# RMS norms of a two-layer diffusion backbone: the reciprocal root moved from the operand to the matmul result

## The reference, cut to what matters

```
rmsnorm(x, g)  = x * rsqrt(mean(x*x) + EPS) * g
modulate(x)    = rmsnorm(x, g) * (1 + scale) + shift      # scale, shift: one value per channel and group
proj           = modulate(x) @ w_in
conv_ffn       = (silu(g) * v) @ w_down,  g, v = split(dwconv3(modulate(x) @ w_up) + conv_b)
```

## Time and profile before

| | before |
|---|---|
| time, median of 3 runs | 2189.38 us (2186.27 to 2192.53) |
| profiled execution: span, first to last instruction | 2179.9 us |
| PE busy | 1991.0 us (91%) |
| DVE busy | 1154.7 us (53%) |
| POOL busy | 1152.3 us (53%) |
| ACT busy | 670.4 us (31%) |

### The profile page before, as it was taken

How to read it: one execution, slowest core, us unless ns; L and a number is a source line. 1 busy time by engine, 2 the same in 40 slices (tenths; PEclk the granted TensorE clock), 3 DMA queues, 4 the chain that set the end, 5 groups by cost and what they waited for, 6 DMA issues and landing times. The chain is left out here.

```text
span 2179.9 us, 33056 instructions
## 1 busy us (share of the span) xinstructions
PE 1991.0 (91%) x12945; PEld 1864.4 (86%) x12945; DVE 1154.7 (53%) x1505; ACT 670.4 (31%) x1093; POOL 1152.3 (53%) x437
## 2 busy tenths in 40 slices
PE   5789887989999999998999999997697999999997
PEld 3678776878899889997998999896696999999997
DVE  4655575667634653354647676768614452452353
ACT  4334332233211320121356464647201220120121
POOL 3233323535567556776454444440474777777763
PEclk8899988989999999999999999998798999999999
DMA  8211116524434522224143333322321222222221
GB/s 275 100 45 53 36 34 209 183 92 144 151 110 124 155 87 68 74 59 128 39 120 116 97 106 97 101 75 87 107 68 48 68 73 72 77 67 78 68 63 73
DMA packets 292913, 208.60 MB, mean 96 GB/s; under 512 B 7344, under 2 KB 284885, under 8 KB 292309
## 3 DMA queue, kind: packets, MB, share of 16 engines
q1 hardware_dynamic: 292821, 207.32, 31.2%
HBM read 196.63 MB, written 10.67 MB: 95 GB/s over the span
## 5 line engine op out<-in xcount | busy, mean ns | idle before, releaser
L828 POOL TENSOR_SCALAR w_hi<-raw 128x1024 fp32r<-128x1024 f32 (+1 forms) x216 | 629.7, 2915 | 983.5 <-PE ps L859 909.8
L859 PE MATMUL ps<-h_hi,w_hi 128*128 128x322 f32 (+1 forms) x2304 | 559.9, 324 | 22.3 <-DVE h_lo L1702 22.0
L859 PE MATMUL ps<-h_lo,w_hi 128*128 128x322 f32 (+1 forms) x2304 | 533.8, 313 | 0.0
L859 PE MATMUL ps<-h_hi,w_lo 128*128 128x322 f32 (+1 forms) x2304 | 533.1, 313 | 0.0
L831 POOL TENSOR_TENSOR w_lo<-raw,w_hi 128x1024 fp32r<-128x1024 f32 (+1 forms) x216 | 522.2, 2418 | 18.0
L859 PEld LDWEIGHTS ps<-h_hi,w_hi 128*128 128x128 f32 x2304 | 391.2, 192 | 51.0 <-issue 33.4
L859 PEld LDWEIGHTS ps<-h_hi,w_lo 128*128 128x128 f32 x2304 | 394.5, 191 | 0.0
L859 PEld LDWEIGHTS ps<-h_lo,w_hi 128*128 128x128 f32 x2304 | 391.5, 191 | 0.0
L859 PE MATMUL ps<-g_hi,w_hi 128*128 128x322 f32 (+1 forms) x816 | 190.4, 315 | 10.3 <-DVE g_lo L1956 10.3
L859 PE MATMUL ps<-g_lo,w_hi 128*128 128x322 f32 (+1 forms) x816 | 188.7, 313 | 0.0
L859 PE MATMUL ps<-g_hi,w_lo 128*128 128x322 f32 (+1 forms) x816 | 188.2, 312 | 0.0
(11 more groups left out here) (295 smaller groups left out, 2533.2 us busy)
## 6 DMA issues: line engine op xcount, KB each, us to landing
ada<-in_ada_w SPq DMA_DIRECT2D x48, 1024.0 KB, 5.3
raw<-in_ffn_w_up SPq DMA_DIRECT2D x88, 512.0 KB, 3.9
raw<-in_ssd_w_in SPq DMA_DIRECT2D x40, 512.0 KB, 4.1
R<-scr_acs SPq DMA_DIRECT2D x40, 512.0 KB, 4.8
raw<-in_ffn_w_down SPq DMA_DIRECT2D x32, 512.0 KB, 3.8
raw<-in_att_w_in SPq DMA_DIRECT2D x16, 512.0 KB, 6.1
raw<-in_ssd_w_out SPq DMA_DIRECT2D x16, 512.0 KB, 4.0
raw<-in_ffn_w_down SPq DMA_DIRECT2D x16, 384.0 KB, 3.4
```

The source lines that it names most:

```text
L828: nc.gpsimd.tensor_scalar(w_hi[j % 2][:, 0:k, :], raw[j][:, 0:k, :], 1.0, None, ALU.mult).then_inc(w_hi_done, 1)
L859: ins = mm(out[:, cols], w[slot][:, k, :], x[:, k_of(k), cols], start=first and k == 0 and i == 0, stop=last and k == n - 1 and i == 2)
```

## The change

- The root no longer goes into h. `h_hi` = x * gain (ScalarE, `high`) and `h_lo` = x * gain - h_hi (VectorE, `low`) are written behind each residual update. The root is broadcast into an SBUF row (`rrow`) and multiplied onto the matmul result.
- The two pad columns move together to columns 128 and 129 and hold the shift of the two groups, so that two columns of each result are `shift @ w`. The eviction adds them: as bias of the middle tap or silu, while the side taps see `-shift @ w` in the pads.
- `ss` now runs after k-step 5 of the projection's first tile, `norm_rb` after k-step 3 of its second one (in attention: halfway through the first).
- Evictions: in attention q, k, v are read by VectorE (times root) and then ScalarE adds the bias in SBUF; in FFN and SSD VectorE first scales the slot in place (`scale`), copies two pad columns and forms two biases, and only then ScalarE reads it, in two instructions instead of one.
- The modulation steps are reordered (`ADA_ORDER`), gains are formed pair by pair. `high` and `low` of norm 0 stand inside the chain of steps 1 to 7. Step 8's weights are no longer loaded early but after attention, and step 9's behind the read-back of `xT`. Steps 16 to 19 move to output tiles 4 and 5.
- SSD: the dt work moves by about one tile, state and y updates are done in PSUM or in place instead of over a temporary (`y2`).

```diff
-W = NP_ + 1 + NS + 1
+W = NP_ + 2 + NS
-S0 = NP_ + 1
+S0 = NP_ + 2
+PADS = slice(NP_, S0)
+ADA_ORDER = (4, 5, 6, 7, 0, 1, 2, 3, 8, 16, 9, 17, 10, 18, 11, 19, 12, 13, 14, 15)
-        ADA_B = ((8, 9), (10, 11), (12, 13), (14, 15), (16,), (17,), (18,), (19,))
+        ADA_B = ((8, 9), (10, 11), (12, 13), (14, 15), (16, 17), (18, 19), (), ())
...
-    put(0, 1, "dtT", 0)
-    put(3, 1, "sum", 0)
-    put(4, 1, "acsT", 0)
+    put(2, 0, "dtT", 0)
+    put(4, 1, "sum", 0)
+    put(5, 1, "acsT", 0)
...
@@ SyncE, behind attention
+            ada(8)
+            sp.dma_start(xT[:, :, :], scr_x).then_inc(x_back, 16)
             ada(9)
-            sp.dma_start(xT[:, :, :], scr_x).then_inc(x_back, 16)
...
@@ TensorE, FFN
+                            def row(k, half=half):
+                                if half == 0 and k == 5:
+                                    ss(n_)
+                                if half == 1 and k == 3:
+                                    norm_rb(n_)
...
@@ ScalarE
+            def high(n, k):
+                act.wait_ge(gain_done, k // 2 + 1 + 4 * n if n < 2 else 7 + n)
+                hi, _ = h_at_k(n, k)
+                for s_, cols in SEGS:
+                    ins = A_(hi[:, cols], xT[:, k, cols], ACT.Copy, scale=gain1[:, n, k, s_:s_ + 1])
+                ins.then_inc(h_hi_done, 1)
             for s in range(1, 8):
                 ada_high(s)
+                if 2 <= s < 6:
+                    high(0, 2 * (s - 2))
+                    high(0, 2 * (s - 2) + 1)
...
-                            act.wait_ge(mm_done, 2 * i + (tp + half + 1))
+                            act.wait_ge(ffn_v, 2 * i + (2 * f0 + half + 1))
...
-                            A_(buf[:, :], acc(half), ACT.Identity, bias=param_at(m + bcol),
-                               scale=param_at(m + (wc + 44))).then_inc(ffn_id, 1)
+                            for s_, cols in ((0, slice(0, S0)), (1, slice(S0, W))):
+                                b_ = 24 + 2 * half + s_
+                                ins = A_(buf[:, cols], acc(half)[:, cols], ACT.Identity, bias=small[:, b_:b_ + 1],
+                                         scale=param_at(m + (wc + 44)))
+                            ins.then_inc(ffn_id, 1)
...
@@ VectorE
+            def low(n, k):
+                dve.wait_ge(gain_done, k // 2 + 1 + 4 * n if n < 2 else 7 + n)
+                dve.wait_ge(h_hi_done, 8 * n + k + 1)
+                hi, lo = h_at_k(n, k)
+                for s_, cols in RANGES:
+                    ins = stt(lo[:, cols], xT[:, k, cols], gain1[:, n, k, s_:s_ + 1], f32(hi[:, cols]), ALU.mult,
+                              ALU.subtract)
+                    (step(ins) if s_ == 0 else ins.then_inc(h_ready, 1))
+            def scale(slot, n):
+                step(tt(acc(slot), acc(slot), rrow(n)[:, :], ALU.mult))
+                step.wait()
+            def side_pads(slot):
+                step(cp(acc_wide(slot)[:, 0:W + 2:W + 1], acc(slot)[:, PADS]))
             for s in range(1, 8):
                 if s < 7:
                     ada_low(s + 1)
                 ada_row_out(s)
                 mod_evac(s - 1, 0)
+                if s < 5:
+                    gain(0, s, slice(2 * s - 2, 2 * s))
+                if 2 <= s < 6:
+                    low(0, 2 * (s - 2))
+                    low(0, 2 * (s - 2) + 1)
...
+                        tt((q_raw, k_raw, v_raw)[i][:, :], src, rrow_att[:, :], ALU.mult).then_inc(acc_free_dve, 1)
...
+                            dve.wait_ge(mm_done, 2 * i + (tp + half + 1))
+                            if isinstance(i, int) and (p, i, half) == (0, 0, 0):
+                                row(n_)
+                            scale(half, n_)
+                            side_pads(half)
+                            ts(small[:, 24 + 2 * half:26 + 2 * half], acc(half)[:, PADS], nw, pcol_at(m + bc_), ALU.mult,
+                               ALU.add).then_inc(ffn_v, 1)
                             dve.wait_ge(ffn_id, 2 * i + (2 * f0 + half + 1))
...
@@ VectorE, SSD y update
-                        tt(h64(y2[:, :]), h64(bank(b)), per_head(eacs, c, d_, g), ALU.mult).then_inc(ssd_free_dve, 1)
-                        ins = tt(y_, y_, y2[:, :], ALU.add)
+                        chain(tt(h64(bank(b)), h64(bank(b)), per_head(eacs, c, d_, g), ALU.mult))
+                        tt(y_, y_, bank(b), ALU.add).then_inc(ssd_free_dve, 1)
```

More of the change, by code:

```diff
@@ L849, in _, with steps @@
             mm, tr = nc.tensor.matmul, nc.tensor.transpose
-            def steps(t, slot, aslot, x_hi, x_lo, ks, k_of=lambda k: k, first=True, last=True, n=KD, ready=None):
+            def steps(slot, aslot, x_of, ks, first=True, last=True, n=KD, ready=None, after=None):
                 out = acc(aslot)
@@ L966, in _ @@
                         pe.wait_ge(x_spilled, 16)
-                    ins = steps(t, t % 2, t % 2, h_hi, h_lo, (2 * q, 2 * q + 1), ready=h_wait(0) if t == 0 else None)
+                    if t == 0 and q == 2:
+                        norm_rb(0)
+                    ins = steps(t % 2, t % 2, h_of(0), (2 * q, 2 * q + 1), ready=h_wait(0) if t == 0 else None)
                     if q == 3:
@@ L1074, in pair @@
                             pe.wait_ge(acc_free_dve, dve_accs(ap) + 2 * i + half - 2)
-                            steps(t, half, half, h_hi, h_lo, range(KD),
-                                  ready=h_wait(n_) if peeled and p == 0 and half == 0 else None
-                                  ).then_inc(mm_done, 1)
+                            begins = peeled and p == 0
+                            def row(k, half=half):
[3 more added lines that the diff above has]
+                                    norm_rb(n_)
+                            steps(half, half, h_of(n_), range(KD), ready=h_wait(n_) if begins and half == 0 else None,
+                                  after=row if begins else None).then_inc(mm_done, 1)
                             if ada:
@@ L1121, in y_part @@
                         pe.wait_ge(*acc_free(A_O + half - 2))
-                    ins = steps(None, half, half, y_hi, y_lo, (k % KD,), k_of=lambda _: k, first=part == 0,
-                                last=part == 1)
+                    ins = steps(half, half, y_of(part), (k % KD,), first=part == 0, last=part == 1)
                     if k % KD == KD - 1:
@@ L1266, in so_pair @@
                             pe.wait_ge(acc_free_dve, 2 * i + (half + dve_accs(A_O) - 2))
-                        steps(None, half, half, y_hi, y_lo, range(KD), k_of=lambda k: 8 * part + k, first=part == 0,
-                              last=part == 1).then_inc(mm_done, 1)
+                        steps(half, half, y_of(part), range(KD), first=part == 0, last=part == 1).then_inc(mm_done, 1)
             for k in range(12, 16):
@@ L1609, in _ @@
             A_(small[:, 8:13], small[:, 0:5], ACT.Sqrt).then_inc(yr_root, 1)
-            def so_squares(i):
-                for half in range(2):
-                    square(3, 2 * i + half, (so_x, 2 * i + (half + 1)), sq[half][:, :])
-            so_squares(0)
-            with act.Fori(1, 4) as i:
-                so_squares(i)
-            norm(3)
+            act.wait_ge(x_back, 32)
+            for hi, i, _, _, k0, k1 in H2_PADS:
+                ins = A_(hi[:, i:i + k1 - k0, PADS], mod[:, 72 + k0:72 + k1, :], ACT.Copy)
+            ins.then_inc(shift_hi, 1)
+            for m in range(KD):
+                square(3, m, (so_x, m + 1), sq[m % 2][:, :], before=True)
+                if m == 7:
+                    A_(h_hi[:, 7, PADS], mod[:, 79, :], ACT.Copy).then_inc(shift_hi, 1)
+            root(3)
             ffn(1, T_F1, A_F1)
@@ L2212, in _ @@
+            low(3, 7)
+            dve.wait_ge(shift_hi, 5)
+            tt(h_lo[:, 7, PADS], mod[:, 79, :], f32(h_hi[:, 7, PADS]), ALU.subtract).then_inc(shift_lo, 1)
             add_square(3, 7, sq[1])
-            norm(3)
             ffn(1, T_F1, A_F1)
```

520 lines of the change are left out of this document (314 added, 206 removed).

## The result

After: 2217.72 us median of 4 runs (2212.05 to 2218.10); before, on the same chip: 2187.82 us (2179.93 to 2192.53). The ratio is 1.0133, 95% interval 1.0112 to 1.0153. I had forecast 2174 us and a range up to 2198: wrong in sign and outside the range. The profiled execution took 2217.51 us with a span of 2215.7. So only 1.8 us lie around a span; most of the 9.5 us that the prediction put there was that the profiled execution of before was a short one.

A forecast was written before the change was run, and what follows sets the result against it. TensorE, 91% busy, was taken to bound the kernel with its dense work plus holes. Terms -38.8 + 3 + 6.5 + 3 + 0 + 11 = -15.3 us gave 2174 us, own range 2164 to 2184, 8 in 10 2155 to 2198.

The forecast's parts named there:

- Norms 1 to 3: TensorE's holes at these norms mostly close, as h is written behind each residual: 13.5, 10.8 and 14.5 us won, together -38.8.
- the hole only moves: Rival at the norms: the second tile waits for the broadcast as the first did; 2184 us, chance 0.11.
- Norm 0 and its chain: Start of the kernel: no gain, first tile ends near 93 against 89.9; term +3 us, bounds -12 and +8.
- Steps 8 and 9: Modulation behind attention: weights land later, step 9's behind the read-back of `xT`; term +6 us, bounds 0 and +10.
- Steps 16 to 19: Modulation steps run in pairs; term +0.5 us.
- Attention: Evictions: VectorE gets 12 scalings of about 0.86 us, partly hidden; term +3 us, bounds 0 and 10.
- FFNs: Evictions take 1.5 us longer per tile, hidden with 7.1 to spare; term 0 for 44 pairs.
- the cover of `hm`: FFN pairs with modulation keep 0.5 us of cover; rival that it fails: +18 us, 2192 us, chance 0.10.
- SSD: Net 64 us more on VectorE, mostly hidden; 3 us in each of three groups plus 2 us: +11, bounds -5 and +32.
- in-order waits between VectorE and ScalarE at each conv tile: Rival in SSD: they put half of the 64 us on TensorE's path, +32; 2197 us, slower, chance 0.15.
- the 14.7 us credited for the lock: SSD y update: VectorE no longer held by GpSimd's lock, 32 x 0.46 = -14.7 us of its work.
- waits for freed slots over 20 us: Sign against the forecast: it fails as a whole if PE's waits for freed slots sum to more than 20 us.

The follow-up runs named there:

- tenth run: The changed kernel with VectorE's scaling, side pads and bias left out in the second FFN; median 1.3 us below the changed kernel's.
- twelfth run: The kernel before with only the y update multiplied in place in PSUM; 2182.65 us beside 2185.84 for before, ratio 0.9987.
- fourth: The changed kernel with norm 2 alone done as in the kernel before, but the dt chain's polynomial one tile later than there; 25 us less.
- fifth run: The changed kernel with norm 2 and the dt chain as in the kernel before, and modulation steps 16 to 19 spread; 2176.6 us.
- third: The changed kernel with VectorE's two side taps of each SSD conv tile, from the second group on, behind the next scan work; 3.4 us more.
- sixth: The changed kernel with the SSD dt chain moved later, off the first conv tiles; 6 us less by medians.
- seventh: The changed kernel with the side taps of the b and c tiles alone put behind the next scan event; 7.8 us less by medians.
- eighth run: The changed kernel with steps 16 to 19 spread, the dt chain later, and the b and c taps behind the next scan event; 2201.0 us.

## Why the prediction was wrong

- *Norms 1 to 3*: right. Forecast -38.8; measured -12.7, -13.9 and -14.6, -41.2 in all. That norm 1 came within 1 us of its forecast is partly luck: it holds 4.2 us at tiles 26 to 28 for which seven other kernels with the same code there have 0.6, and 9.1 us at tiles 59 to 65, where its modulation pair now stands, for which the prediction had 3. That the hole only moves is refuted by norm 3's two waits of 2.29 and 1.68 us.
- *Norm 0 and its chain*: the steps were right, the end a little off. `ada_hi(3)` to (6) were forecast at 47.0, 54.1, 61.1 and 68.1; they started at 45.7, 53.6, 60.3 and 67.0; the timeline of ACT has the period with the two pairs of `high`:

```profile
45.72 1.89 ACT L1402 ACTIVATE ada_hi<-ada 128x2048 fp32r<-128x2048 f32 x1
51.77 1.92 ACT L1430 ACTIVATE h_hi<-xT,gain 128x128 fp32r<-128x128 f32 x4 [4.16 <-DVE gain L1785]
53.60 1.90 ACT L1402 ACTIVATE ada_hi<-ada 128x2048 fp32r<-128x2048 f32 x1
```

  The last turn started at 79.0 for 81 to 82, and tile 0 ended 0.7 us earlier than before, not 3 later; since tile 0 lies between -2.9 and +4.2 us in the other kernels, +3 is not refuted.
- *Steps 8 and 9*: right (+6.8 for +6), with the cause that was named: putting step 9 ahead of the read-back removed the jump at tile 17, though 4.3 us came back at the next one.
- *Steps 16 to 19*: the term of +0.5 failed, at +12.6. I counted the steps' work and not their transfers' due times: a pair was already the tightest pattern at output tiles 1 to 3, and two more pairs in a row left no tile in which the two buffers could refill. Spreading them took 8.8 of the 12.6 us away.
- *Attention*: -1.2 for +3. The same code cost +5.3 us in four other kernels, so this term is neither shown right nor wrong.
- *FFNs*: the cover of `hm` held through 44 pairs (lag flat), but the term of 0 is 10.5 us in the profile (3.9 and 6.6), at first tiles and passes between parts. The 2.2 us of tiles 65 to 91 repeat in every changed kernel; much of the rest comes and goes between kernels with the same code there. What the tenth run shows to be the scaling's, 2.0 us at tile 150, lies in norm 3's stretch, where the prediction had 1.7 for it.
- *SSD*: the term that decided. Its mechanism stood in the prediction as a rival: in-order waits between VectorE and ScalarE at each conv tile, which decides once more than 26 of the 64 us show. Of the stage's 49 us, 37.5 went with the scaling. (The rival's sum is 8.7, not 8.6, and gives 2198 us, not 2197.) These sizes were off. First, "3 us of PE waits in each of three groups": a group cost 11.4 us on average, since lateness goes on from the b tile to the x tiles (6.0, 6.6 and 5.4 us at the border and 4.4, 4.4 and 3.3 on the next three tiles), where I counted one border. Second, the slow matmuls behind each wait, 2.3 us of a border's 6.0, were in no term. Third, the 14.7 us credited for the lock bought nothing in the kernel before (twelfth run), and with the scaling 12.2 of them came back on two neighbours. And "2 us where the dt chain meets the first tiles" was 14.9: 5.4 went with the scaling, and putting the chain's series back by one tile took 10.4 off the first tiles (fourth to fifth run). Its pieces moved one tile later, which the diff shows and I read as harmless.

So the step that failed is the prediction's "there I expect 3 us of PE waits in each of three groups; plus 2 us where the dt chain meets the first tiles": +11 us, where the runs show 49, the scaling 37.5 of them and the places of the dt chain most of the rest. How the 37.5 split into added work and a longer way through each eviction stays open.

The error of 51 us (forecast -15.3, measured +35.8 by spans) is SSD 38, steps 16 to 19 12, FFNs 10.5, less 9 us by which start, attention and norms went better.

What the prediction named as tests came out so: no wait over 3 us between the last output tile and the third tile at norms 1 to 3 (1.8, 0.9 and 2.3 us at most, right), `ss` inside the first tile (right), the last turn after 80 us (79.0, just wrong), one PE wait for `ada_lo` near 345 of more than 10 us (8.6, just wrong), `hm` ending as before relative to `w_lo` (0.69 us behind its end for 0.68, right). As to the sign against it, waits for freed slots over 20 us would refute the forecast: they hardly occurred (3.4 us on `cg`, 0.9 on `bT`), and the forecast failed all the same, through the conv results and scan banks that VectorE delivers late. That test looked at the wrong resource.

## What to carry to other kernels

Before work is moved onto an engine, add up its work and its waits between the two points where another engine takes something from it, not over the stage: at 65% busy on average VectorE had no room for a group's added scalings and waits. Where it has none, reordering may only hand lateness on: the four reorderings tried here (third, sixth, seventh and eighth run) won back 3.2 of the stage's 49 us at best. One change can be right at some of its places and wrong at another, and the parts should be tried apart: norms 0, 1 and 3 new and norm 2 old, with the dt chain in its old places, steps 16 to 19 spread and step 9 earlier, is 0.7% faster instead of 1.3% slower. A moved step brings its transfer's due time with it: ask when its buffer comes free and how long the load takes.

## What the hardware showed that I had not expected

- A gap of a few microseconds on TensorE can be paid twice. Behind a gap of 4.1 us, pairs of 322-column matmuls ran at 0.74 us for 0.46, and the stretch's granted clock was 0.82; also at norm 3 behind 2.29 us of waiting and 1.27 us of ten one-column matmuls. Behind gaps of 0.90 us (before, at the border) and 1.68 us (after, norm 3) the next pair took 0.53 and 0.56 us and those behind it 0.46 and 0.47: they did not slow.
- An in-place VectorE multiply in PSUM, 128x642, takes 0.83 us, between the bounds of 0.689 and 1.01 taken from neighbours (the prediction took 0.87).
- An instruction that is no longer held up by GpSimd can leave the cost in place. In the kernel before the y update in PSUM took 14.7 us off its line, and VectorE as a whole did 11.2 us less over tiles 92 to 131. In the changed kernel two neighbours with two SBUF inputs took 7.9 and 4.3 us more; without the scaling they did not.
- GpSimd is held up as well: `w_hi` takes 2.77 us, and 3.90 when it starts beside VectorE's `ada_lo`.
